# Splitting the first two refills of a loop body in a streamed mixture-of-experts kernel, and moving half a gather and the bias products

## What is computed

```python
def body(e, acc):
    gu = t @ w_gu[e] + b_gu[e]
    g, u = jnp.split(gu, 2, axis=-1)
    g = jnp.minimum(g, SWIGLU_LIMIT)
    u = jnp.clip(u, -SWIGLU_LIMIT, SWIGLU_LIMIT)
    hdn = (u + 1.0) * (g * jax.nn.sigmoid(SWIGLU_ALPHA * g))
    y = hdn @ w_dn[e] + b_dn[e]
    return acc + comb[:, e][:, None] * y
```

## Time and profile before

| what | value |
|---|---|
| median of 3 runs | 1296.98 us (1295.6 to 1298.13) |
| profiled execution, its own time | 1298.09 us |
| its span | 1296.3 us |
| PE busy | 1221.3 us (94%) |
| DVE, ACT, POOL busy | 408.7, 172.2, 33.0 us |
| moved by DMA | 475.73 MB, mean 367 GB/s |
| share of 16 DMA engines taken by SP's and ACT's queue | 87.3% |

### The profile page before, as it was taken

The page is one execution under the profiler, slowest core; times in us unless marked ns, Lnnn a source line. Parts: engine busy times, 40 slices in busy tenths (PEclk is TensorE's granted clock), DMA queues, the critical chain, the costliest instruction groups (busy, mean ns, idle before and its releaser), DMA issues.

```text
span 1296.3 us, 13989 instructions
## 1 busy us (share of the span) xinstructions
PE 1221.3 (94%) x5550; PEld 579.1 (45%) x5550; DVE 408.7 (32%) x774; ACT 172.2 (13%) x311; POOL 33.0 (3%) x50
## 2 busy tenths in 40 slices
PE   5999999999999999999999998989999998989996
PEld 1777478887543243334334333433333332333432
DVE  5178895884422211120221102120311211120212
ACT  3222004231221010010101001000100010010100
POOL 3300100001000000000000000000000000000000
PEclk9999999999999999999999999999999999999998
DMA  9943442879499999999999999999999999999994
GB/s 375 383 168 116 145 164 98 312 286 399 164 374 424 388 428 429 429 429 429 429 429 428 429 428 429 428 429 429 429 428 429 429 429 429 428 429 428 427 427 174
DMA packets 49362, 475.73 MB, mean 367 GB/s; under 512 B 3905, under 2 KB 4065, under 8 KB 22706
## 3 DMA queue, kind: packets, MB, share of 16 engines
q1 hardware_dynamic: 48082, 471.26, 87.3%
q0 software_dynamic: 1248, 4.03, 0.9%
HBM read 474.22 MB, written 1.05 MB: 367 GB/s over the span
## 4 chain that ended last, share of the span: by engine, by line
PE 68%; DMA 23%; DVE 4%; ACT 2%; issue 1%; SPq 0%; ACTq 0%; DVEq 0%
PE bank L1136 21%; PE bank L1182 15%; DMA ring_sb<-w_down 13%; PE bank L836 10%; DMA ring_sb<-w_gu 9%; PE bank L1081 4%; PE bank L997 3%; PE bank L1198 3%; PE bank L845 3%; PE bank L1026 2%; PE bank L1095 1%; DVE area_sb L2056 1%; DVE area_sb L1800 1%; ACT area_sb L1442 1%; PE bank L761 1%
## 5 line engine op out<-in xcount | busy, mean ns | idle before, releaser
L1136 PE MATMUL bank<-ring_sb,area_sb 128*64 128x512 f32 x1536 | 400.2, 598 | 13.9 <-DMA ring_sb<-w_gu 13.9
L1136 PEld LDWEIGHTS bank<-ring_sb,area_sb 128*64 128x64 f32 x1536 | 124.9, 137 | 223.0 <-issue 213.2
L1182 PE MATMUL bank<-ring_sb,area_sb 128*64 128x512 f32 x640 | 175.5, 603 | 8.2 <-DMA ring_sb<-w_down 8.2
L1136 PE MATMUL bank<-area_sb 128*64 128x512 f32 x512 | 171.2, 594 | 0.0
L836 PE MATMUL bank<-area_3h_sb,ring_sb 128*128 128x256 f32 x704 | 154.2, 379 | 0.0
L836 PEld LDWEIGHTS bank<-area_3h_sb,ring_sb 128*128 128x128 f32 x704 | 133.2, 190 | 20.1 <-issue 1.8
L2056 DVE TENSOR_SCALAR area_sb<-bank 128x512 f32<-128x512 f32 x32 | 22.0, 688 | 319.1 <-PE bank L1136 319.1
L2080 DVE TENSOR_TENSOR area_sb<-area_sb,bank 128x512 f32<-128x512 f32 x64 | 44.0, 688 | 211.8 <-PE bank L1198 211.8
L2087 DVE TENSOR_TENSOR area_sb<-bank,area_sb 128x512 f32<-128x512 f32 x32 | 22.1, 692 | 220.1 <-PE bank L1182 220.1
L1182 PEld LDWEIGHTS bank<-ring_sb,area_sb 128*64 128x64 f32 x640 | 54.0, 138 | 82.7 <-issue 82.4
L1451 ACT ACTIVATE area_sb<-area_sb 128x512 f32<-128x512 f32 x32 | 20.1, 630 | 504.2 <-DVE area_sb L2056 504.2
(11 more groups left out here) (276 smaller groups left out, 799.8 us busy)
## 6 DMA issues: line engine op xcount, KB each, us to landing
ring_sb<-w_gu SPq DMA_DIRECT2D x96, 2048.0 KB, 25.5
ring_sb<-w_down SPq DMA_DIRECT2D x40, 2048.0 KB, 25.5
area_sb<-w_gu SPq DMA_DIRECT2D x32, 2048.0 KB, 28.4
area_sb<-w_down SPq DMA_DIRECT2D x16, 2048.0 KB, 20.1
ring_sb<-w_in SPq DMA_DIRECT2D x14, 2048.0 KB, 9.8
ring_sb<-w_ada SPq DMA_DIRECT2D x12, 2048.0 KB, 10.2
area_3h_sb<-w_down SPq DMA_DIRECT2D x8, 2048.0 KB, 35.4
ring_sb<-w_branch SPq DMA_DIRECT2D x3, 2048.0 KB, 9.4
```

Of the source, the lines that this page charges most:

```text
L1136: ins = pe.matmul(bank[n][r, :], xT[:, k, r], w[e][:, n * 512:(n + 1) * 512], start=False, stop=k == KT - 1, skip_group_check=True)
L1182: ins = pe.matmul(bank[4 + n][r, :], hidT[:, k, e * SLOTS:(e + 1) * SLOTS], w[e][:, kk, n * 512:(n + 1) * 512], start=False, stop=k == KT ...
```

## The change

Four things are changed.

- A new semaphore `first_rows_used` is raised by the last matmul of row block 0 of pair a. Chunks 9 and 10 are each loaded in two pieces of 1 MB (128 rows of 8 KB): the first pieces of both wait for row block 0, the second pieces for row block 1 as before. The first pieces raise semaphores of their own (`early_landed`), for which the matrix engine waits as well before it uses chunks 9 and 10.
- In pair a, the second half of the gather stands between row blocks 1 and 2.
- In pair a, `gate_bias` stands between the first half of the gather and row block 0, in every body.
- It goes away from its former places: in the router for the first body, and behind pair b's `down` for the others.

```diff
@@ -515,6 +517,8 @@
         def wait_moe_chunk(eng, i, b, c):
             n = PAIR_CHUNKS * b + c
+            if n in (9, 10):
+                eng.wait_ge(early_landed[n - 9], i * 16 + 16)
@@ -606,12 +610,29 @@
+            def load_split(i, j):
+
+                for part in range(2):
+                    for n in (9, 10):
+                        e = n % 2
+                        row = 4 * P * (n - 9)
+                        src = a["w_down"][0, bass.ds(j * 4 + e, 1), row:row + 4 * P, :]\
+                            .rearrange("e (p k) m -> p (e k) m", k=4)[:, 2 * part:2 * part + 2, :]
+                        dst = moe_slot(0, n)[:, 2 * part * D:2 * (part + 1) * D].rearrange("p (k m) -> p k m", k=2)
+                        if part == 0:
+                            sp.wait_ge(first_rows_used, i + 1)
+                            sp.dma_start(dst, src).then_inc(early_landed[n - 9], 16)
+                        else:
+                            wait_slot(i, n)
+                            sp.dma_start(dst, src).then_inc(moe_chunk_landed(0, n), 16)
+
             def body(i, j, last):
-                for n in range(MOE_SLOTS, BODY_CHUNKS):
+                load_split(i, j)
+                for n in range(MOE_SLOTS + 2, BODY_CHUNKS):
                     load(i, j, n)
@@ -1100,7 +1121,6 @@
                 pe.wait_ge(bias_landed, 16 * 6)
-                gate_bias(0, 0, 0)
                 rank(0)
@@ -1117,9 +1137,13 @@
                 if b == 0:
                     pe.wait_ge(member_ready, (i + p) * 2 + 2)
-                for g in range(2):
+                for g in range(1 + b):
                     gather(i, s, b, g)
+                if b == 0:
+                    gate_bias(i, p, 0)
                 for k in range(KT):
+                    if b == 0 and k == 2:
+                        gather(i, s, b, 1)
@@ -1138,6 +1162,8 @@
                             if k % 2 and n == 3 and (e == 0 or k < KT - 1):
                                 ins.then_inc(weights_used, 1)
+                            elif b == 0 and k == 0 and n == 3 and e == 1:
+                                ins.then_inc(first_rows_used, 1)
@@ -1207,20 +1233,16 @@
                     if b == 0:
                         gate_bias(i, p, 1)
-                    elif not last:
-                        gate_bias(i + 1, p, 0)
```

More of the change, by code:

```diff
@@ L446, in build_layer @@
         weights_used = sem("weights_used")
+        first_rows_used = sem("first_rows_used")
+        early_landed = [sem(f"early_landed{i}") for i in range(2)]
         gate_up_done = sem("gate_up_done")
@@ L1209, in body, with one_pass @@
                         gate_bias(i, p, 1)
-                    elif not last:
-                        gate_bias(i + 1, p, 0)
                 for n in range(4):
                     scatter(i, "b", 1, n)
-            def one_pass(p, first=False):
-                if not first:
-                    gate_bias(p * BODIES, p, 0)
+            def one_pass(p):
                 with pe.Fori(0, BODIES - 1) as j:
@@ L1222, in _ @@
             router()
-            one_pass(0, first=True)
+            one_pass(0)
             pe.wait_ge(flag_ready, 1)
```

## The result

Over 17 runs each, the changed kernel takes 1299.3 us (1296.88 to 1301.62) and the kernel before 1296.98 us (1294.44 to 1299.12). The ratio is 1.0017, with a 95% interval from 1.001 to 1.0024: slower by 2.2 us (1.3 to 3.1). The middle of that is inside the 2.6 us that the prediction had called no change, and the time is 0.3 us from its 1299.0. The profiled execution took 1297.84 us for a span of 1296.1, less than that of before (1298.09): one execution does not rank the two.

A forecast was written before the change was run, and what follows sets the result against it. The DMA stream from chunk 19 of body 0 was taken to bound the kernel, its start set by the matrix engine; 1.07 + 0.14 + 0.15 + 0.65 = +2.0 us gave 1299.0 us, range 1296.6 to 1301.6.

The forecast's parts named there:

- the path of body 0: Matrix engine's work up to chunk 19's release in body 0: bias, split gather and wait for the copy, 1.36 us.
- The early refill: Chunks 9 and 10 of body 0: earlier first pieces fill the first DMA hole, the second grows equally; counted 0.
- The bias products: Pair a of body 0: four matmuls are new work ahead of chunk 19's release, +1.07 us; their removal from the router, 0.
- The split gather: Pair a of body 0: one more change of matmul kind, +0.14 us, and row block 0's wait for the copy, +0.15.
- The rate of the pieces: Chunks 9 and 10 of bodies 1 to 7: 8 KB rows instead of 16 KB load slower, +0.65 us.
- The pieces "have long landed" at `down`: At `down`, the matrix engine's two more semaphores cost nothing, since the pieces are there already; 0.
- The end of the other bodies: Later bodies: scatters start 1.07 us sooner, bias returns behind the gather; body length unchanged but for 0.14 us.
- no third hole: Later bodies: DMA queue stays full, with 4.6 us of reserve in body 1; the contrary rival had a chance of 0.04.
- the 851 that the prediction named as a sign of being wrong: Stretch from chunk 19 of body 0 on: expected 848 to 850 us; longer than 851 us would refute the forecast.
- two in a row: Scatters between bodies: two take about 1.05 us, four 3.98, read as already waiting for the vector engine's additions.
- The end is the release of chunk 19 plus 173 chunks, plus a fixed tail: Whole loop: end follows from chunk 19's start in body 0, then 173 chunks at 4.90 us each and a constant tail.
- The prediction's own test on the issue of chunk 19: Body 0: issue expected between 426.8 and 427.4 us instead of 425.75; at 425.8 or sooner the forecast is wrong.

The follow-up runs named there:

- only_gather: The kernel before, with only the second gather half of pair a moved behind row block 1; ratio to the kernel before 0.9998 (0.9989 to 1.0007).
- only_bias: The kernel before, with only the bias products moved, behind the whole gather of pair a; ratio to the kernel before 0.9994 (0.9985 to 1.0003).
- only_split: The kernel before, with only chunks 9 and 10 in two pieces each, first pieces behind row block 0; ratio to before 1.0016 (1.0007 to 1.0025).
- late_split: The kernel before, with chunks 9 and 10 in two pieces each, all four behind row block 1; ratio to before 1.0017 (1.0008 to 1.0027).
- bias_back: The changed kernel, with pair a's bias products back in their former places; ratio to the kernel before 1.0014 (1.0005 to 1.0023).
- late_b: The kernel before, reordered in pair b, with second gather half and scatters deferred to row blocks 4 and 5; ratio to before 0.9996 (0.9987 to 1.0005).
- before_again: The kernel before, unchanged, profiled once more in one execution; no timed ratio, first gather matmul of body 0 at 359.91 us.
- after_again: The changed kernel, unchanged, profiled once more in one execution; no timed ratio, first gather matmul of body 0 at 362.12 us.
- both: The changed kernel, with second gather half and scatters deferred in pair b too, pair a's bias back in place; ratio to before 1.0015 (1.0005 to 1.0024).
- pair_b: The kernel before, with the reordering in pair b, second gather half and scatters behind row block 1; ratio to before 1.0 (0.9991 to 1.0009).
- down_rows: The kernel before, with every `w_down` chunk in two transfers of 128 rows of 8 KB; ratio to before 1.0035 (1.002 to 1.005).

## Why the prediction was right, and where it was not

The time, the range and the sign came out as forecast. That the number fits so well is in good part luck. The prediction built its 2.0 us from 1.36 of the path of body 0 and 0.65 of the pieces. Alone, the path costs nothing that can be measured (only_gather and only_bias, with upper ends of +0.9 and +0.4 us), and the pieces cost the whole 2 us (only_split and late_split). By steps:

- **The early refill brings 0.** Right: only_split and late_split have the same Z and the same time. The first hole went, a smaller one of 1.6 us came ahead of chunk 11, which the prediction had not listed, and neither mattered.
- **The bias products, +1.07.** Wrong in this place. The step failed at "in pair a of body 0 they are new work". Alone, behind the whole gather, they do add 1.08 to X (only_bias). Behind half a gather they fill a wait for the copy of 1.18 us (bias_back), and add nothing.
- **The split gather, +0.29.** It is the whole of X: +1.61 in only_gather, since without 2 us of gather the table load ahead of the copy is bare. The prediction had both rows, the copy's end at 365.15 and the gather's half at 364.04, and charged the wait only from the end of the bias. The sum of the two steps, 1.36 against 1.60 measured, is near by luck, because each hides in the other; the division was wrong.
- **The rate of the pieces, +0.65.** The mechanism was right and the size too small: 1.0 to 1.5 us of Z for 14 chunks, 5.0 for 60, so 0.08 us for each and not 0.046. The uncut figure of the 8 KB row at 421 GB/s, 1.3 us, was the better one; it was halved since a packet more or less per engine was said to move it by 2%, where it is 5% (16 packets of 8 KB in 2.52 MB). The figures quoted there from the Trainium skill (DMA: Bandwidth & Descriptors, "Anatomy of one DMA" and "Bandwidth") are measured on transfers issued from GpSimd; SP issues these, and 60 further ones cost 5.0 us of Z here, and not 120. Whether the length of the rows or the count of transfers costs it is open.
- **The pieces "have long landed" at `down`, 0.** Wrong from the middle of the loop on. In body 0 it holds, but once the stream is what the matrix engine waits for, chunk 9 lands behind a piece of chunk 10, and the engine waits 3.3 us ahead of `down` of pair a. This term was put at nothing, and it is likely the second microsecond of what the pieces cost.
- **The end of the other bodies, no third hole.** Right: Z grows by the pieces alone. At 851.4 us in the first profile it is past the 851 that the prediction named as a sign of being wrong, at 850.8 in the second it isn't. One row was misread: the "two in a row" of about 1.05 us are the two records of one scatter. Two scatters take 2.04 us (late_b), so four take their 3.98 us without losing time to a wait. No term hung on it.
- **The end is the release of chunk 19 plus 173 chunks, plus a fixed tail.** This is the weakest step. Over single profiles the stream adds up: Z is within 0.3 us of 849.9 in every kernel that leaves pair b and the transfers alone. But an earlier release is hardly passed on (3.08 us in, about 0.5 out at the last packet of late_b), and the tail isn't fixed: the prediction took it that the matrix engine waits for the last packet. It has about 1.1 us in hand there (the wait in before_again), less than a drop of the clock costs or than work moved behind its last waits. In the profiles of before, after_again, bias_back, only_split, late_split, late_b and both it doesn't wait.

X and Y together, from the first gather matmul to the last half of `down`, fit the timed runs better than X and Z. The kernel before has 914.8 and 916.2 us in its two profiles. only_bias (915.4), only_gather (916.2), pair_b (915.7) and late_b (915.1) lie within 0.1 us of that range, and no loss of time shows in them; the changed kernel (917.7 and 918.5), bias_back (918.4), only_split (918.6), late_split (918.9) and down_rows (919.3) lie above, and they are slower. Only "both" falls out of line (916.3, and +1.9 us of time). So +1.08 of X in only_bias was measured against an X of 63.69, while the same kernel has 65.34 in its other profile: the three profiles with the gather of pair a unsplit that keep the full clock in the front all have a drop in body 0 instead. How often that happens, no run tells, and with one or two profiles per kernel the parts can't be added up to better than about a microsecond.

The mean granted clock is not what the pieces cost. It is about 0.98 in the runs with pieces of chunks 9 and 10 and 0.988 in those of only_bias and late_b, but only_gather has 0.982 and loses nothing, and down_rows has 0.99 with 60 split chunks and is the slowest of these.

No kernel tried here beats the kernel before.

The prediction's own test on the issue of chunk 19 (wrong at 425.8 or sooner) was badly put: an absolute time also holds the front's scatter of 2 us. The first profile gave 425.64 and the second 427.42, for the same X.

## What to carry to other kernels

Before an earlier end of the transfers is counted as a gain, look whether the last engine still waits for them there, and by how much: here it had 1.1 us in hand. When a transfer is cut in pieces, write down the order in which they land, and ask which use needs which: a piece of the next chunk between two pieces of this one delays this one. When work moves away from between a producer's result and its use, price the whole chain that it covered, a table load too, and not the instruction that takes its place. In this loop, which transfers bound, pieces of half the row length cost 1.7% of their own time (0.08 of 4.90 us), and that was more than their earlier start was worth.

## What the hardware showed that was not expected

- Two transfers of 64 partitions in place of one of 128 halve the rate while they run (218 GB/s at a DMA share of 1.01) and cost this kernel 430 to 500 us.
- The granted clock falls to half for 3.4 us at a time, at places that differ between executions of one kernel. The one at 1267.35 in the kernel before comes with a wait of the matrix engine of 1.30 us, the one at 395.34 in before_again with one of 1.27 us. One in the front, near 93 us, shifts the start of body 0 by 1.65 us.
- A full queue of DMA engines doesn't end together: 1.6 us (before) and 2.4 us (late_b) pass between most engines' last packet and the very last one.
